# First attention of a two-block fp32 network: packed values, and the softmax shares applied to the heads' outputs

## The reference

```python
def block_fn(args):              # one block of 128 queries
    ...                          # score, top 256 of the causal keys
    logits = einsum("bthd,btkd->bhtk", q_b, k_sel) * HEAD_DIM ** -0.5
    logits = logits + bias       # T5 bucket bias
    p = softmax(logits)
    o = einsum("bhtk,btkd->bthd", p, v_sel)
```

## Time and profile before

| | us |
|---|---|
| median of 3 runs | 2590.57 (2590.13 to 2590.76) |
| span of the profiled execution | 2590.4 |
| TensorE matmul busy | 2485.7 (96%) |
| TensorE weight load busy | 2054.2 (79%) |
| DVE / ACT / POOL busy | 1683.1 / 950.8 / 658.6 |
| chain that ended last | TensorE 85%, DVE 8%, ACT 3% |

### The profile page before, as it was taken

How to read it: one execution, slowest core, us unless ns; L and a number is a source line. 1 busy time by engine, 2 the same in 40 slices (tenths; PEclk the granted TensorE clock), 3 DMA queues, 4 the chain that set the end, 5 groups by cost and what they waited for, 6 DMA issues and landing times.

```text
span 2590.4 us, 32111 instructions
## 1 busy us (share of the span) xinstructions
PE 2485.7 (96%) x12208; PEld 2054.2 (79%) x12208; DVE 1683.1 (65%) x2874; ACT 950.8 (37%) x1766; POOL 658.6 (25%) x536
## 2 busy tenths in 40 slices
PE   7899999988999999999999998999999999999998
PEld 5688888777787788888888886888877787888987
DVE  4599999477425898888654449585687556004843
ACT  5521212487224332222312144332333236226842
POOL 3157421576542100000000130000000035334753
PEclk9999999899999999999999999999999999999999
DMA  5112333100544365664533141323237223542242
GB/s 188 33 42 66 98 98 98 41 1 20 175 167 128 107 192 179 197 185 139 188 117 134 37 143 57 106 86 102 98 131 267 82 72 127 175 134 91 103 162 99
DMA packets 264324, 302.11 MB, mean 117 GB/s; under 512 B 11272, under 2 KB 216556, under 8 KB 264172
## 3 DMA queue, kind: packets, MB, share of 16 engines
q1 hardware_dynamic: 263860, 299.96, 35.6%
q10 hardware_dynamic: 312, 0.09, 0.0%
HBM read 228.15 MB, written 70.29 MB: 115 GB/s over the span
## 4 chain that ended last, share of the span: by engine, by line
PE 85%; DVE 8%; ACT 3%; issue 1%; DMA 1%; POOL 1%; SPq 0%; DVEq 0%; ACTq 0%; POOLq 0%
PE ps L67 82%; PE ps L70 3%; DVE sm L79 1%; DVE tmp L76 1%; ACT tmp L73 1%; ACT pth L73 1%; DVE pwa L76 1%; DVE wl L76 1%; DVE B2l L76 1%; DVE tmp L79 0%; DVE ptl L79 0%; DVE X L79 0%; ACT wh L73 0%; DVE pwb L76 0%; DVE XO L79 0%
## 5 line engine op out<-in xcount | busy, mean ns | idle before, releaser
L76 POOL TENSOR_TENSOR wl<-raw,wh 128x512 fp32r<-128x512 f32 (+1 forms) x224 | 294.4, 1335 | 1560.7 <-ACT wh L73 1560.6
L73 ACT ACTIVATE wh<-raw 128x512 fp32r<-128x512 f32 (+1 forms) x388 | 226.4, 621 | 238.1 <-PE ps L67 175.2
L67 PE MATMUL ps<-B2h,wh 128*128 128x512 f32 x616 | 243.0, 394 | 8.8 <-DVE tmp L76 7.7
L67 PE MATMUL ps<-B2l,wh 128*128 128x512 f32 x616 | 241.0, 391 | 0.0
L67 PE MATMUL ps<-B2h,wl 128*128 128x512 f32 x616 | 240.8, 391 | 0.0
L73 ACT ACTIVATE tmp<-ps 128x512 f32<-128x512 f32 (+5 forms) x161 | 116.9, 738 | 298.3 <-PE ps L67 283.9
L73 ACT ACTIVATE wh<-ws 128x512 fp32r<-128x512 f32 x152 | 94.4, 627 | 295.6 <-DVE ws L76 268.3
L67 PE MATMUL ps<-ah,wh 128*128 128x512 f32 (+1 forms) x608 | 193.0, 394 | 9.3 <-DVE al L76 5.1
L76 DVE TENSOR_TENSOR tmp<-tmp,ps 128x512 f32<-128x512 f32 x204 | 138.5, 684 | 84.9 <-PE ps L67 66.9
L67 PE MATMUL ps<-B3h,wh 128*128 128x512 f32 x448 | 178.3, 398 | 15.2 <-DVE B3l L76 7.0
L67 PE MATMUL ps<-al,wh 128*128 128x512 f32 (+1 forms) x608 | 190.9, 391 | 0.0
(11 more groups left out here) (295 smaller groups left out, 5767.2 us busy)
## 6 DMA issues: line engine op xcount, KB each, us to landing
ada<-in_ada_w SPq DMA_DIRECT2D x48, 512.0 KB, 3.6
raw<-in_w_in SPq DMA_DIRECT2D x37, 512.0 KB, 4.4
raw<-in_a_w_in SPq DMA_DIRECT2D x33, 512.0 KB, 4.7
gates<-tmp SPq DMA_DIRECT2D x32, 512.0 KB, 3.0
raw<-in_w_ffn_gate SPq DMA_DIRECT2D x24, 512.0 KB, 5.3
hd<-tmp SPq DMA_DIRECT2D x22, 512.0 KB, 4.2
gf<-hd SPq DMA_DIRECT2D x22, 512.0 KB, 7.2
raw<-in_a_w_out SPq DMA_DIRECT2D x20, 512.0 KB, 4.0
```

The lines of the kernel that those rows point to most:

```text
L67: return self.e.matmul(*a, **k) if self.e else Ins()
L73: return self.e.activation(*a, **k) if self.e else Ins()
L76: return self.e.tensor_tensor(*a, **k) if self.e else Ins()
```

## The change

The value tile is packed: `VS` holds v_hi in columns 0 to 63 and v_lo in columns 64 to 127 of one stationary operand. `values` now runs once for a pair of items n−1, n: V_packed·P_hi and V_packed·P_lo, two matmuls per key block instead of three, and 256 columns hold two heads instead of sharing the bank between four. Rows 0 to 63 of the output hold the part of v_hi, rows 64 to 127 that of v_lo. `stored` copies the whole output to SBUF (`OS`) on ACT, and `folded` on DVE adds the two halves across, an add of 64x128 for each head of the pair, into `OT`.

`norm` is gone. The weights stay exp values. One reciprocal for eight heads is taken (`share`), POOL spreads it to 128x512 (`spread`), TensorE turns that with four transposes in the ring of the turns (`shares`), ACT copies it to `RS` (128x512), and POOL multiplies `OT`'s eight heads of the query block by it in place (`scaled`, 128x512), once per block.

The lags become: TensorE (0 score), (3 turn), (5 shares), (5 values part 1), (4 values part 0); ACT (6 stored), (3 turned), (0 exps), (5 shares), (4 conv); DVE (6 folded), (0 far), (2 share), (0 near), (3 turned); POOL (-2 near), (4 spread), (8 scaled). The zero fill of `vp` on POOL and the second pair of value copies go.

```diff
@@ pe_attend
         def turn(n):
-            e.wait_ge(*self.at("soft", n))
+            e.wait_ge(*self.at("exp", n))
...
+        def shares(n):
+            b, hd = self.ITEMS1[n]
+            if hd < 7:
+                return
+            p = self.take(e, ("r", b), ring=self.p_turn)
+            e.wait_ge(*self.at("spread", b))
+            for i in range(4):
+                c = slice(i * 128, i * 128 + 128)
+                ins = e.transpose(p[:, c], self.RB[:, c], self.ident[:, :])
...
             for i in (range(mid, b + 1) if part else range(mid)):
-                c, c2 = slice(i * 128, i * 128 + 128), slice(i * 256, i * 256 + 256)
-                ins = self.prods(e, po[:, 0:256], (V[0][:, c], V[1][:, c]), (PH[:, c2], PL[:, c2]),
-                                 odd == 0 and i == 0, odd == 1 and i == b)
+                V, c2 = self.VS[:, i * 128:i * 128 + 128], slice(i * 256, i * 256 + 256)
+                e.matmul(po, V, PH[:, c2], start=i == 0, stop=False)
+                ins = e.matmul(po, V, PL[:, c2], start=False, stop=i == b)
...
-        pipeline(64, [(0, score), (4, turn), (6, lambda n: values(n, 1)), (5, lambda n: values(n, 0))])
+        pipeline(64, [(0, score), (3, turn), (5, shares), (5, lambda n: values(n, 1)), (4, lambda n: values(n, 0))])
@@ act_attend
+                e.activation(self.RS[:, :], self.ps(("r", b)), ACT.Copy).then_inc(
+                    self.sig["evac"].up(("shared", b), ("free", ("r", b))), 1)
...
+            if n % 2:
+                p = n // 2
+                e.wait_ge(*self.at("pv", p))
+                e.activation(self.OS[p % 2][:, :], self.ps(("o", p))[:, 0:256], ACT.Copy).then_inc(
+                    self.sig["evac"].up(("ocopy", p)), 1)
...
-        pipeline(64, [(4, turned), (2, norm), (7, stored), (0, exps), (4, conv)])
+        pipeline(64, [(6, stored), (3, turned), (0, exps), (5, shares), (4, conv)])
@@ dve_attend
+        def folded(n):
+            if n % 2:
+                (b, hd), p = self.ITEMS1[n], n // 2
+                o = self.OT[:, hd // 2 * S + b * 128:hd // 2 * S + b * 128 + 128]
+                po, s = self.ps(("o", p)), self.OS[p % 2]
+                e.wait_ge(*self.at("ocopy", p))
+                e.tensor_tensor(o[0:64, :], po[64:128, 0:128], s[0:64, 0:128], ALU.add)
+                e.tensor_tensor(o[64:128, :], po[0:64, 128:256], s[64:128, 128:256], ALU.add).then_inc(
+                    vec.up(("fold", p), ("free", ("o", p))), 1)
...
-        pipeline(64, [(0, top_far), (2, norm), (0, top_near), (4, turned)])
+        pipeline(64, [(6, folded), (0, top_far), (2, share), (0, top_near), (3, turned)])
@@ pool_attend
+        def scaled(n):
+            b, hd = self.ITEMS1[n]
+            if hd == 7:
+                o = self.OT[:, :].rearrange("p (j t) -> p j t", j=4)[:, :, b * 128:b * 128 + 128]
+                e.wait_ge(*self.at("fold", n // 2))
+                e.wait_ge(*self.at("shared", b))
+                e.tensor_tensor(o, o, self.RS[:, :].rearrange("p (j t) -> p j t", j=4), ALU.mult).then_inc(
+                    self.sig["gps"].up(("ot", b)), 1)
...
-        pipeline(64, [(-2, near), (2, norm)])
+        pipeline(64, [(-2, near), (4, spread), (8, scaled)])
...
-    ATTENDED = (("pv", 31), ("ot", 15), ("pl", 63))
+    ATTENDED = (("pv", 31), ("ot", 7), ("pl", 63))
```

More of the change, by code:

```diff
@@ L1720, in pe_values_pads, with value_parts, act_values @@
         ins.then_inc(self.sig["prod"].up(("prod", key)), 1)
-    def value_pads(self, key, pads, row):
+    def value_parts(self, key, row):
         v = self.ps(key)[:, :].rearrange("p (i c) -> p i c", c=128)[:, :, row:row + 64]
-        for n, (H, L, c) in enumerate(((pads[0], pads[1], 0), (pads[2], pads[3], 64))):
-            yield n, v, *(x[:, :].rearrange("p (i c) -> p i c", c=128)[:, :, c:c + 64] for x in (H, L))
-    def act_value_pads(self, e, key, pads, row, after):
+        VS = self.VS[:, :].rearrange("p (i c) -> p i c", c=128)
+        return v, VS[:, :, 0:64], VS[:, :, 64:128]
+    def act_values(self, e, key, row, after):
+        v, hi, lo = self.value_parts(key, row)
         e.wait_ge(*self.at("prod", key))
@@ L1730, in act_value_pads, with dve_values @@
             e.wait_ge(*self.at(*event))
[L1731 to L1745, removed]
+        e.activation(hi, v, ACT.Copy).then_inc(self.sig["ahi"].up(("vhi", key)), 1)
+    def dve_values(self, e, key, row):
+        v, hi, lo = self.value_parts(key, row)
+        e.wait_ge(*self.at("vhi", key))
+        e.tensor_tensor(lo, v, hi.bitcast(F32), ALU.subtract).then_inc(
+            self.sig["vlo"].up(("vlo", key), ("free", key)), 1)
     def pe_attend(self, e):
@@ L1777, in turn @@
                 ins.then_inc(self.sig["prod"].up(*marks), 1)
+        def shares(n):
[7 more added lines that the diff above has]
+                ins = e.transpose(p[:, c], self.RB[:, c], self.ident[:, :])
+            ins.then_inc(self.sig["prod"].up(("prod", ("r", b))), 1)
         def values(n, part):
             b, hd = self.ITEMS1[n]
-            if n % 4 < 2:
+            if n % 2 == 0:
                 return
[L1784 to L1790, removed]
+            p = n // 2
+            if part == 0:
+                self.take(e, ("o", p), ring=self.p_out)
+            po = self.ps(("o", p))[:, 0:256]
+            PH, PL = self.pt1[p % 2]
+            for event in (("vlo", "v1"), ("pl", n - 1), ("pl", n)):
                 e.wait_ge(*self.at(*event))
@@ L1829, in act_attend, with shares @@
     def act_attend(self, e):
[L1830 to L1835, removed]
+        def shares(n):
+            b, hd = self.ITEMS1[n]
+            if hd == 7:
+                e.wait_ge(*self.at("prod", ("r", b)))
+                if b:
+                    e.wait_ge(*self.at("ot", b - 1))
+                e.activation(self.RS[:, :], self.ps(("r", b)), ACT.Copy).then_inc(
+                    self.sig["evac"].up(("shared", b), ("free", ("r", b))), 1)
         def turned(n):
-            e.wait_ge(*(self.at("pv", self.pv(n - 4)) if n >= 4 else self.at(*self.PROJECTED)))
+            e.wait_ge(*(self.at("pv", n // 2 - 2) if n >= 4 else self.at(*self.PROJECTED)))
             for part, PH, PL, src in self.turned1(n):
@@ L1896, in dve_attend, with share @@
         vec = self.sig["vec"]
[L1898 to L1901, removed]
-            e.wait_ge(*self.at("exp", n))
-            e.reciprocal(rs, sm).then_inc(vec.up(("share", n)), 1)
+        def share(n):
+            b, hd = self.ITEMS1[n]
+            if hd == 7:
+                e.wait_ge(*self.at("exp", n))
+                if b > 1:
+                    e.wait_ge(*self.at("spread", b - 2))
+                e.reciprocal(self.st8(b, 3), self.st8(b, 2)).then_inc(vec.up(("share", b)), 1)
         def top_far(n):
```

49 lines of the change are left out of this document (23 added, 26 removed).

## The result

The changed kernel takes 2612.04 us (median of 4 runs, 2611.38 to 2612.96) against 2590.66 for the kernel before (2590.13 to 2592.7). The ratio is 1.0078, with a 95% interval of 1.0066 to 1.0091. The forecast was 2586.1 with a range of 2577 to 2595. It was wrong in its sign and missed its range by 17 us. The profiled execution has a span of 2610.1 us against 2590.4.

What follows compares the result with a forecast made beforehand. TensorE, 96% busy, heads the chain, but after the change a ring through ACT and DVE sets the pace: −7.5 us up to the last turn, +3 at the end, so 2590.4 − 4.5 + 0.2 = 2586.1 us, range 2577 to 2595.

Steps and rivals of the forecast that it cites:

- the ring is open: At b = 0 and 1, pairs use half the score banks, so no closed ring; items 0 to 15 forecast at −1 us.
- ring S: Not in the prediction; named in the experiments: value matmuls, scores, turn, pth, exp, output copy, folds, next value matmuls, through output's half bank.
- the signs that were named for being wrong: Folds over 0.3 us each, DVE's wait for ACT's copy over 0.8 us per pair, or no such wait.
- The waits of TensorE that were to show the ring: TensorE was to wait before scores for near, the subject of a sign listed for checking the forecast; no size given.
- TensorE's own work: 144 value matmuls go at 0.12 us each, 17.3 us; 32 transposes add 3.5; TensorE has 13.8 us less to do.
- Ring T: Near, exp, output copy, folds, far, near; sets the pace at 6.0 us per pair at b = 7, 5.4 at b = 6.
- The folds: Two DVE adds per pair, taken as 0.42 us; bounds 0.3 if they overlap and 0.6 if not.
- The removed reciprocals: DVE loses a reciprocal per item between far and near, worth 0.15 us at most.
- Rival 3: TensorE stays at 1.2 GHz 10 us longer in b = 0 to 2, costing 4 us: 2590; chance 12%.
- Rival 2: Fold wait on DVE between folded and far: copy seen 0.5 us later per pair, 26 pairs, +13, about 2597; chance 15%.
- The tail: End of the stage, last turn to TensorE resuming on cl3: about 18 us against 15.3, costing +3 us.
- 1.2 us more than the forecast: At the stage's end, scaled would wait for DVE's cl0 by the skill's rule: total 2587.3, left out of the forecast.

Runs made afterwards that it cites:

- e5: Changed kernel with the folds moved to the end of DVE's step, ACT's copy left behind the exp: 2675.87 us, ratio 1.0329.
- e2: Changed kernel with two half banks for the outputs and two instead of three for the turns: 2604.26 us, ratio 1.0059.
- e1: Changed kernel with ACT's output copy one step earlier, ahead of the exp, and the folds last in that step on DVE: 2594.96 us, ratio 1.0015.
- e7: e1 with half banks by stage: two output and two turn up to b = 3, one and three from b = 4: 2587.8 us, ratio 0.9995.
- e4: Changed kernel with the output bank freed by ACT's copy; folds add the copy to itself, so outputs are wrong: 2610.17 us, ratio 1.0081.
- e9: e7 with ACT's convolution copies behind the last output copy, plus six idle transposes per pair in items 0 to 15: 2583.54 us, ratio 0.9971.
- e6: Changed kernel with six unread identity transposes per pair ahead of the value matmuls in items 0 to 15: 2606.21 us, ratio 1.0057.
- e10: Kernel before the change with six unread identity transposes per pair ahead of the value matmuls in items 0 to 15: 2589.26 us, ratio 0.9993.

## Why the prediction was wrong, step by step

**The failed step: "At b = 0 and 1 a pair has one part and uses only half the banks, so the ring is open", and with it the walk through one ring alone.** I walked what waits for score banks and didn't ask who frees the output's. The code of the change has the answer in one mark: `("free", ("o", p))` is on the second fold. The prediction's own stretches run from `ptl` to `ptl`. The rows of the kernel after for item 16, the first, and item 56, the last of them:

```profile
528.83 0.55 DVE L79 SCALAR_TENSOR_TENSOR ptl<-ps,pth 128x384 fp32r<-128x384 f32 x1
...
641.32 1.28 DVE L79 SCALAR_TENSOR_TENSOR ptl<-ps,pth 128x512 fp32r<-128x512 f32 x2
```

| items | up to 16 | 16 to 23 | 24 to 31 | 32 to 47 | 48 to 55 | 56 to the last turn | sum |
|---|---|---|---|---|---|---|---|
| forecast, new minus old | −1 | +1 | 0 | −4.8 | −3.6 | −1 | −9.4 |
| measured | +7.2 | +6.6 | +3.1 | +0.9 | −0.7 | −0.3 | +16.8 |

(The starts of `ptl` of items 24, 32 and 48 are 549.86, 570.14 and 615.48.) At items 0 to 15, where only TensorE's matmuls were to shrink, it cost 7.2 us. e5 and e2 show ring S; e1 and e7 together take it away as the bound and give back 24 us.

None of the signs that were named for being wrong came: a fold takes 0.29 us, not over 0.3, and DVE's wait for `os` is 0.55 us a time (15.3 in 28), not over 0.8. The waits of TensorE that were to show the ring, before scores for near, are in no row. It waited for `ot`, which was not on the list.

**TensorE's own work.** Right. The matmuls went as counted, and the others follow each other at the pitch taken: at the end of the stage, 664.74 to 665.45, six intervals take 0.71 us, 0.12 each. But the gain of 13.8 us was booked against a TensorE that can start its value matmuls whenever it likes.

**Ring T.** Right in kind, short in size, and wrong as the only one. The pitches of the kernel after are 4.9, 5.3, 5.7, 6.0 and 6.6 us per pair at b = 3 to 7, and e4 shows ring T at 5.8 to 6.4 at b = 6, where 5.4 was forecast. In e1, e7 and e9 the forecast pitches appear within 0.2 us from b = 3 to 7, but as those of another bound, and the agreement is in part luck: there DVE's sum of folds, far, near and `ptl` sets them. The walk at b = 7 had one `ptl` of 1.2 us and 1.6 for exp, copy and hand-over; DVE's sum has a second `ptl` in place of that 1.6.

**The folds.** The rows of the tile (durations in ns, least, median, most):

```profile
L76 DVE TENSOR_TENSOR ot<-ps,os x64: 283/288/294, 500.6 to 669.2; 64x128 f32<-64x128 f32 x64
L73 ACT ACTIVATE os<-ps x32: 363/376/392, 500.2 to 668.5; 128x256 f32<-128x256 f32 x32
```

Half the partitions cost what all cost in the earlier trace rows. The two starts are 0.31 apart, and far follows 0.62 behind the first, where I took 0.42. The bound of 0.6 for "they don't overlap" was the right end: 0.2 us per pair, or some 5 us in the pairs with two parts. Those are 24 (b = 2 to 7), where the prediction counted 26. The removed reciprocals gave nothing: far's start to near's start is still 0.85 (596.74 to 597.59), as the 0.83 of the earlier trace rows.

**The clock.** Rival 3 was right in kind and too small. I had it 10 us longer at a cost of 4; it was 24 us longer (538 against 514), and e6 gives 5.8 us back. It is also not independent of the ring: the low clock lengthens TensorE's part in ring S (2.15 us per turn at b = 0 at 0.50, 1.32 at 1.00 in e6). That the gaps in ring S bring the low clock fits the rows, but no run shows it by itself.

**Rival 2, the slower one,** put the price at DVE between folds and far with 0.5 us for each pair with two parts, 2597 in all (its own terms, 2586.1 + 13, make 2599). The price came out at up to 1.7 us per pair (6.6 for four), and highest in the early columns, pairs of one part among them. A wait between two engines costs most where there is least work to cover it; I had reasoned the other way.

**The tail.** Right in its sum. The end of the stage in order of time on all engines:

```profile
660.95 1.29 SPq L109 DMA_DIRECT2D tmp<-cv  x3
...
668.02 0.58 ACT L73 ACTIVATE rs<-ps 128x512 f32<-128x512 f32 x1
...
668.90 0.59 DVE L76 TENSOR_TENSOR ot<-ps,os 64x128 f32<-64x128 f32 x2 [5.84 <-ACT os L73]
669.52 3.44 DVE L76 TENSOR_TENSOR cl<-tmp,ch 128x1024 fp32r<-128x1024 f32 x2
669.57 2.31 POOL L76 TENSOR_TENSOR ot<-ot,rs 128x512 f32<-128x512 f32 x1 [9.42 <-DVE ot L76]
...
672.01 6.51 POOL L76 TENSOR_TENSOR cl<-tmp,ch 128x1024 fp32r<-128x1024 f32 x2
```

```profile
678.67 0.70 PE L67 MATMUL ps<-ch,wh 128*128 128x512 f32 x2 [1.69 <-POOL cl L76]
```

TensorE resumes 17.7 us after the last turn (forecast 18), and the end costs 2.9 (forecast 3). The terms were off in opposite ways: the last of the loads had landed 6.1 us after the last turn instead of 8, `scaled` took 2.31 us instead of 1.34, and POOL's cl2 and cl3 took 6.51 instead of 5.67. TensorE's gap ahead of cl0 was 5.2 us where 8 was forecast; behind it the clock stood at 0.50 (670 to 674), as forecast. The same multiplication began 0.8 us ahead of DVE's subtractions in e9 and took this:

```profile
641.95 1.27 POOL L76 TENSOR_TENSOR ot<-ot,rs 128x512 f32<-128x512 f32 x1 [6.70 <-DVE ot L76]
642.78 2.65 DVE L76 TENSOR_TENSOR cl<-tmp,ch 128x1024 fp32r<-128x1024 f32 x2 [0.91 <-ACT ch L73]
```

So the order of the starts decides who pays. In the kernel after DVE's first `cl` began 0.05 us ahead of POOL's multiplication and took its usual time, and POOL's took 1.0 more; DVE's second `cl` then took 2.30, until POOL was through (DVE's row of the tile; the earlier trace rows has 2.36 for both):

```profile
L76 DVE TENSOR_TENSOR cl<-tmp,ch x2: 1226/1761/2296, 669.5 to 670.7; 128x1024 fp32r<-128x1024 f32 x2
```

The Trainium skill, SBUF — State Buffer, section "Who interferes with whom", says that a DVE instruction with two SBUF inputs contends with a GpSimd instruction that reads SBUF. By that rule I had given 1.2 us more than the forecast; the rows show 1.0 on `scaled`, so the trace agrees, and I should have put it into the sum.

**What stays open.** How the 19.7 us divide between ring S and the low clock can't be settled to the microsecond, since the clock lengthens the ring: e6 takes the low clock away first and gives 5.8, e9 takes it away last and gives 4.4. e1 moves the copy and the folds together; the copy ahead of the exp with the folds left at the head of the next step wasn't run. Whether more output banks at b = 4 to 7 would help wasn't tried beyond e2, since turns and scores use what there is.

## What to carry to other kernels

When a result is taken out of its bank more often, write down for every bank the step in which it is taken, the step in which it is freed, and who frees it; if both are the same step of in-order queues, every engine between them forms a ring. A copy that a bank's release waits for goes ahead of the long operation in its queue, not behind it: here the place of a copy of 0.38 us, with its folds, decided 17 us. And saved instructions on the busiest engine were worth nothing in the stretches where it waited, least of all in the short items at the start, where its clock stood low for 24 us longer as well.

## What the runs showed of the chip that I had not expected

- TensorE stood at a granted clock of 0.50 for 36 us (502 to 538), in which it was busy for 2.5 to 4.0 us of every 4 and never waited longer than 1.7 us for the folds. With six transposes of 128 columns per pair that nobody reads the clock was 1.00 from 502 (e6) or 506 (e9, e10) on, as long as they lasted. The kernel was 5.8 us shorter with the ring and 4.4 us shorter without it; the kernel before gained 1.4 us, which can't be told from nothing.
- A DVE addition of 64x128 with one input in PSUM takes 0.288 us, as long as a `ptl` of 128x128 (0.29): half the partitions save nothing. A `ptl` of 128x256 takes 0.42 and one of 128x384 0.56, so by my estimate 128 columns are worth 0.13 us and the other 0.16 doesn't depend on the size.
- A DVE instruction with two SBUF inputs and a POOL instruction on SBUF that meet cost the one that begins later about the time of the overlap, in the rows here. POOL's multiplication of 128x512 took 1.27 to 1.29 us in seven blocks and 2.31 when DVE's subtraction had begun 0.05 us ahead. DVE's next subtraction took 2.30 us instead of 1.22, and a fold of e4 that began 0.02 us behind a POOL addition took 0.87 instead of 0.29.
